# Issuing the attention scores of one unit in every step, instead of two units in every second step

## The reference, cut to what matters

```
s = q @ k.T / 8 + bias      # 256 queries x 256 keys, contraction over 64
p = exp(s - max(s));  p = p / sum(p)
o = p @ v
```

## Time and profile before

| | us |
|---|---|
| median of 3 runs | 1029.88 (1029.38 to 1032.31) |
| the profiled execution's own time | 1029.88 |
| its span in the profile | 1028.0 |
| PE busy with matmuls | 1000.3 (97%) |
| PE busy with weight loads, beside the matmuls | 891.3 (87%) |
| DVE busy | 651.1 (63%) |
| ACT busy | 487.7 (47%) |
| share of the DMA queue of the weights in the 16 DMA engines | 50.6% |

### The profile page before, as it was taken

One profiled execution on the slowest core, in us unless ns is written; L12 is line 12 of the kernel. 1 busy time (PEld: TensorE's weight loads), 2 busy tenths in 40 slices (PEclk: granted clock), 3 DMA queues, 4 the chain that ended last, 5 costly groups with the idle time before them and its releaser, 6 DMA issues.

```text
span 1028.0 us, 15335 instructions
## 1 busy us (share of the span) xinstructions
PE 1000.3 (97%) x6174; PEld 891.3 (87%) x6174; DVE 651.1 (63%) x912; ACT 487.7 (47%) x742; POOL 131.7 (13%) x165
## 2 busy tenths in 40 slices
PE   5998999999999999999999999999999999999997
PEld 4886899899999988888889999999887889999995
DVE  4786565754456546675665455447657887757674
ACT  6455354454455333334564454446535455545452
POOL 1510039600002001000010100000550110000000
PEclk9999999999999999999999999999999999999999
DMA  9941345456555653446538645654644364354541
GB/s 345 323 130 41 123 137 192 150 185 214 188 164 167 216 181 99 158 153 216 165 126 284 198 170 191 207 177 135 212 165 156 126 192 134 120 168 124 170 158 41
DMA packets 106837, 174.82 MB, mean 170 GB/s; under 512 B 3984, under 2 KB 66576, under 8 KB 106768
## 3 DMA queue, kind: packets, MB, share of 16 engines
q1 hardware_dynamic: 105280, 172.23, 50.6%
q10 hardware_dynamic: 1488, 1.62, 0.5%
HBM read 172.79 MB, written 1.05 MB: 169 GB/s over the span
## 4 chain that ended last, share of the span: by engine, by line
PE 88%; DVE 4%; DMA 3%; ACT 2%; issue 1%; POOL 0%; ACTq 0%; DVEq 0%; POOLq 0%
PE ps L400 25%; PE ps L345 19%; PE ps L347 18%; PE ps L346 18%; PE ps L508 2%; DMA raw<-in_w_in_e 2%; PE ps L479 1%; PE ps L633 1%; DMA arena<-in_xT 1%; PE ps L491 1%; PE ps L434 1%; DVE arena L1492 1%; DVE wlo L1190 1%; PE ps L621 1%; ACT whi L807 1%
## 5 line engine op out<-in xcount | busy, mean ns | idle before, releaser
L1190 DVE TENSOR_TENSOR wlo<-raw,whi 128x1024 fp32r<-128x1024 f32 (+1 forms) x316 | 373.3, 1220 | 36.7 <-ACT whi L807 16.3
L807 ACT ACTIVATE whi<-raw 128x1024 fp32r<-128x1024 f32 (+1 forms) x316 | 319.6, 1050 | 99.0 <-PE ps L347 57.0
L345 PE MATMUL ps<-hTh,whi 128*128 128x256 f32 (+1 forms) x872 | 248.9, 285 | 3.9 <-ACT whi L807 2.0
L347 PE MATMUL ps<-hTh,wlo 128*128 128x256 f32 (+1 forms) x872 | 246.6, 283 | 0.0
L346 PE MATMUL ps<-hTl,whi 128*128 128x256 f32 (+1 forms) x872 | 246.6, 283 | 0.0
L345 PEld LDWEIGHTS ps<-hTh,whi 128*128 128x128 f32 (+1 forms) x872 | 166.6, 191 | 6.5 <-issue 2.8
L346 PEld LDWEIGHTS ps<-hTl,whi 128*128 128x128 f32 (+1 forms) x872 | 166.7, 191 | 1.2
L347 PEld LDWEIGHTS ps<-hTh,wlo 128*128 128x128 f32 (+1 forms) x872 | 166.6, 191 | 0.0
L345 PE MATMUL ps<-whi,hTh 128*128 128x512 f32 (+1 forms) x368 | 147.7, 401 | 10.4 <-DVE hTl L1440 10.4
L347 PE MATMUL ps<-whi,hTl 128*128 128x512 f32 (+1 forms) x368 | 142.9, 388 | 0.0
L346 PE MATMUL ps<-wlo,hTh 128*128 128x512 f32 (+1 forms) x368 | 142.7, 388 | 0.0
(11 more groups left out here) (165 smaller groups left out, 1031.3 us busy)
## 6 DMA issues: line engine op xcount, KB each, us to landing
raw<-in_w SPq DMA_DIRECT2D x64, 1024.0 KB, 5.6
raw<-in_w_in SPq DMA_DIRECT2D x34, 1024.0 KB, 5.1
raw<-in_w_in_o SPq DMA_DIRECT2D x24, 1024.0 KB, 5.5
raw<-in_w_in_e SPq DMA_DIRECT2D x8, 1024.0 KB, 13.3
raw<-in_w_out_o SPq DMA_DIRECT2D x8, 1024.0 KB, 5.0
raw<-in_w_out_e SPq DMA_DIRECT2D x4, 1024.0 KB, 6.9
raw<-in_w_mem SPq DMA_DIRECT2D x4, 1024.0 KB, 6.0
raw<-in_w_out SPq DMA_DIRECT2D x4, 1024.0 KB, 5.1
```

The lines of the kernel that those rows point to most:

```text
L345: e.matmul(o, a[0], b[0], start=start, stop=False)
L347: return e.matmul(o, a[1], b[0], start=False, stop=stop)
L807: e.activation(split_half(i)[0], raw_half(i), ACT.Copy).then_inc(*up("hi", ("hi", i)))
L1190: e.tensor_tensor(l, raw_half(i), h.bitcast(F32), ALU.subtract).then_inc(*up("lo", ("lo", i)))
```

## The change

PE's program issues the scores of unit s in step s, for every s from 0 to 7. Before, it issued those of the units s and s + 1 together in every even step. Nothing else is changed: the programs of the other engines, the stages of a unit, and the loop of X stay as they are.

```diff
@@ -517,9 +517,8 @@
                     att_transposed(key, s - 2)
                 if 0 <= s - 3 < n:
                     att_values(key, s - 3)
-                if s % 2 == 0 and s < n:
+                if s < n:
                     att_scores(key, s)
-                    att_scores(key, s + 1)
```

## The result

The changed kernel took 1048.49 us (median of 4 runs, 1044.65 to 1050.22) against 1031.04 us (4 runs) for the kernel before. The ratio is 1.0158, with an interval of 1.0134 to 1.0182: 1.6% slower, as forecast. Three executions of the kernel before that lie far out (1104.21, 1243.22 and 5657.68 us, the first two at a mean clock of 0.85 and 0.75) are in none of the ratios of this document. The profiled execution took 1046.09 us with a span of 1044.3 us, 16.3 us longer than the span before.

A forecast was written before the change was run, and what follows sets the result against it. PE was taken as the bound (88% of the chain, no holes in M and D). A 5.2 + B 1.7 + M 3.9 + D 3.9 = 14.7 us on 1029.9 gave 1044.6 us, range 1037 to 1050.

The forecast's parts named there:

- The two units of a pair share four slots, and a unit alone needs all four: PE's scores: a pair runs side by side in 1.07 us, and a unit alone takes about as long.
- The two-slot rival: PE's scores: a unit alone takes two slots, rows of 4 records last 0.65 us, total 1034 us; chance 0.07.
- Weight loads unhidden: PE's scores: a unit alone pays for its weight loads, 24 us more, total 1069 us; chance 0.05.
- 11 wide and 4 narrow splits at 1.19 and 0.74 us, 3.9 us in M and in D, hidden by nothing: Pairs taken apart in four attentions; M and D each have two wide and two narrow, 3.86 us, with no PE hole.
- A + 5.2, with a longer chain at its end: Attention A: four splits, unit 7's scores one step later, end 5.2 us later; last values' wait grows from 0.65 to over 1.
- B + 1.7, step by step: Attention B: three splits, partly covered by PE's waits, so its last values come 1.7 us later.
- the walk: B's steps followed from step 4 at full clock: waits 0.3, 0.3 and 1.2 us before transposes of units 4, 6, 7.
- the sentence on the clock: In B: 3.4 us at the lower clock level lose about 1.7 us, taken as gone after the change.
- 1044.6: Whole kernel: forecast time in us, 1029.9 + 14.7; chance 0.83 for the forecast as worked out.
- My own range: Whole kernel: 1042 to 1048.5 us, from bare splits without B's cover (1045.9) and a second fall of the clock.
- The outer range: Whole kernel: 1037 to 1050 us, from a unit alone cheaper or dearer by up to 0.2 us in 30 units, 6 us.
- a fall of the clock at the end of A: Holes at A's end grow; if B drops to the lower clock again, 1.7 us are not won back: 1046.3 us.

The follow-up runs named there:

- same_rows_pairs: Kernel before, pairs kept, but heads reordered so both units of a pair lie on the same 64 rows; ratio 1.0068 to the kernel before.
- split_B: Kernel before with one unit issued per step in B only, pairs kept in A, M and D; ratio 1.0024 to the kernel before.
- after_again: The changed kernel run again unaltered, in five rounds; ratio 1.0138 to the kernel before, 1043.44 to 1048.73 us.
- fours_MD: Kernel before with the scores of four units issued together in steps 0 and 4 of M and D; ratio 1.01 to the kernel before.
- early_B: Kernel before with B's pairs 2-3, 4-5 and 6-7 issued one step earlier; ratio 1.0058 to the kernel before.
- late_AB: Kernel before with pairs kept but issued one step later in A and B; ratio 1.0279 to the kernel before.
- same_rows_split: The changed kernel with heads reordered so neighbouring units 0-1, 2-3 and so on lie on the same 64 rows; ratio 1.0154 to the kernel before.

## Why the prediction was right

*The two units of a pair share four slots, and a unit alone needs all four.* Right. Alone: 1.06 us. Two units on the same rows: 1.92. DVE's start, on which I based it, holds too: in the changed kernel it starts on unit 7 of A 1.17 us after the unit's scores (82.28 to 83.45), the 1.17 of the pair in the earlier trace rows.

*The two-slot rival* had asked for 0.64 us. Out. *Weight loads unhidden* is out as well: the eight weight loads of a pair are four now, and the spacing of the records is the same.

*11 wide and 4 narrow splits at 1.19 and 0.74 us, 3.9 us in M and in D, hidden by nothing.* Right: 3.83 and 3.96, PE full. Of M's cost, same_rows_pairs shows 2.40 to be the slots and the rest, 1.43, the way into and out of 64-row work.

*A + 5.2, with a longer chain at its end.* 5.26 against the first profile, which happened to be 0.25 us longer in A than five later ones with the same A (37.70 to 37.72); what made it so is open, and split_B has the longer A again (37.99). The last values still wait 0.65 us for ACT; where I expected their wait to grow, the transposes ahead of them wait 0.88.

*B + 1.7, step by step.* 1.66. The waits are where the walk put them (transposes of unit 4, of unit 6, of unit 7):

```profile
109.52 0.63 PE L491 MATMUL ps<-cst,arena 128*128 128x128 f32 x4 [0.24 <-ACT arena L891]
...
114.83 0.63 PE L491 MATMUL ps<-cst,arena 128*128 128x128 f32 x4 [0.27 <-ACT arena L891]
...
117.19 0.66 PE L491 MATMUL ps<-cst,arena 128*128 128x128 f32 x4 [0.86 <-ACT arena L891]
```

0.24, 0.27 and 0.86 us against 0.3, 0.3 and 1.2. What was wrong is the sentence on the clock. "A loss of about 1.7 us, which I take as gone" is 0.54 us (28.04 against 27.50), and it is not in every execution of the kernel before; it was in B in two of three. It did little harm to the sum: the walk sets a B at the full clock against the B of the first profile, so only these 0.54 us are in it. A term built from the sentence would have been three times too large. With both kernels at the full clock, B costs 29.70 - 27.50 = 2.2 us and the four stages 5.5 + 2.2 + 3.8 + 4.0 = 15.5 us.

*1044.6.* The median was 1048.49, which is 3.9 us more. Of these 1.2 us are the kernel before, whose median had risen from 1029.88 to 1031.04 with a fourth run. The ratios give 16.3 and, on the second occasion, 14.2 us, and their intervals hold the 14.7 to 15.5 of the traces. Single executions differ by more than what is left: 1.6 us ahead of A in the first profile, 4.1 us around the start of B in after_again. My own range, 1042 to 1048.5, held by 0.01 us, which is luck; the median of all 39 executions lies 3.1 us above the forecast. The outer range is not quite what its reason gives either: 6 us to either side are 1038.6 to 1050.6, not 1037 to 1050. I had put a fall of the clock at the end of A into the range only, at 1.7 us. That a stretch there can last 13.7 us I had not.

## What to carry to other kernels

Before two small matmuls are moved apart, look whether they run at the same time: where eight records start in twos, the second matmul is free only as long as its partner on the other rows stands next to it. Read the price of a matmul from starts to starts at its two borders; with 0.32, 1.07, 0.65, 0.93 and 0.81 us from one trace the cost of the four splits came out to 0.1 us both in M and in D. And when instructions change places in a program that hands out its banks from a ring, follow the ring for every engine that frees one: in fours_MD and early_B a single wait for a bank (3.46 and 3.81 us) was longer than all that they could have won (1.2 and 1.4), and late_AB had one of 4.5.

## What the runs showed of the hardware that I had not expected

Two matmuls that stand one behind the other on the same rows do not keep those behind them, on the other rows, from starting: the order within a pair made no difference (1.07 us either way, against 1.92 with all four on the same rows).

The lower of the two clock levels came at other places from one execution to the next, in the same kernel, and for 3.4 to 20.5 us at a time. Of three profiles of the kernel before, one had it in B at 103.3, one at 105.3, and one not in B but at 198.9. Behind holes of PE it could last long: 13.7 us in after_again, 44.4 us in four stretches in late_AB. But the same holes did not always bring it: the first profile of the changed kernel has those of after_again and its full clock behind them. What it costs depends on the place: nothing for 3.4 us at the head of B in same_rows_split, 0.54 us for 3.4 us further on in B, where a wait takes up the rest, and 1.5 us for the one at 198.9 (682.50 against 680.97).
